# A two-block transformer on one core: the last 32 tokens of the expert layer gathered row by row, the others computed densely

## The reference, cut to what matters

```python
s1 = einsum('thd,nd->thn', q[..., :half], k1)      # 8 heads, 128 keys on each side
s2 = einsum('thd,nd->thn', q[..., half:], k2)
v1, i1 = top_k(s1, 16);  v2, i2 = top_k(s2, 16)
sc, pos = top_k(all sums v1 + v2, 16)
eidx = (i1 * 128 + i2)[pos]                        # one of 16384 experts
g = softmax(sc)
a = einsum('thkd,td->thk', expert_u[eidx], h)
out = einsum('thk,thkd->td', gelu(a) * g, expert_v[eidx])
```

## Time and profile before

| | us |
|---|---|
| device time, median of 3 runs | 1415.27 |
| lowest and highest of them | 1412.72, 1416.08 |
| device time of the profiled execution | 1414.68 |
| its span | 1412.6 |
| PE busy | 1383.5 (98%) |
| DVE busy | 1006.8 (71%) |
| ACT busy | 692.0 (49%) |
| POOL busy | 392.5 (28%) |

### The profile page before, as it was taken

One profiled execution on the slowest core, in us unless ns is written; L12 is line 12 of the kernel. 1 busy time (PEld: TensorE's weight loads), 2 busy tenths in 40 slices (PEclk: granted clock), 3 DMA queues, 4 the chain that ended last, 5 costly groups with the idle time before them and its releaser, 6 DMA issues.

```text
span 1412.6 us, 28033 instructions
## 1 busy us (share of the span) xinstructions
PE 1383.5 (98%) x11486; PEld 1357.0 (96%) x11486; DVE 1006.8 (71%) x2242; ACT 692.0 (49%) x1188; POOL 392.5 (28%) x185
## 2 busy tenths in 40 slices
PE   6999999999999999999999999999999999999998
PEld 6989899999999999999999999999999899999988
DVE  3573525859998898999966666776667954788743
ACT  5563446544454444444443333333345766656653
POOL 3744467678600000000000000000000553674332
PEclk9998999999999999999999999999999999999999
DMA  8433345555565444444455766556655534555553
GB/s 284 141 103 105 105 133 180 169 165 182 180 204 168 150 149 150 150 149 150 150 174 187 239 184 190 190 185 192 186 188 180 163 122 137 177 165 179 174 171 104
DMA packets 65095, 234.99 MB, mean 166 GB/s; under 512 B 7228, under 2 KB 7612, under 8 KB 64968
## 3 DMA queue, kind: packets, MB, share of 16 engines
q1 hardware_dynamic: 64968, 233.20, 51.8%
HBM read 232.13 MB, written 1.05 MB: 165 GB/s over the span
## 4 chain that ended last, share of the span: by engine, by line
PE 85%; DVE 9%; ACT 4%; issue 1%; DMA 0%; POOL 0%; SPq 0%; DVEq 0%; ACTq 0%
PE PS L551 84%; ACT SPL L991 2%; DVE SPL L1372 2%; DVE ub L2026 2%; DVE ub L2022 1%; DVE ub L2019 1%; PE PS L673 1%; DMA RAW<-in_dense 0%; DVE HF L1389 0%; DVE RS L1384 0%; DVE HS L1394 0%; DVE sb L1953 0%; ACT HS L1016 0%; DVE PS L1415 0%; DVE cosr L1915 0%
## 5 line engine op out<-in xcount | busy, mean ns | idle before, releaser
L991 ACT ACTIVATE SPL<-RAW 128x1024 fp32r<-128x1024 f32 x432 | 456.4, 1058 | 565.3 <-PE PS L551 561.9
L2049 POOL TENSOR_TENSOR SPL<-RAW,SPL 128x1024 fp32r<-128x1024 f32 x149 | 361.0, 2426 | 1000.8 <-ACT SPL L991 1000.7
L551 PE MATMUL PS<-HS,SPL 128*128 128x256 f32 x4656 | 572.8, 282 | 12.8 <-DVE SPL L1372 11.9
L551 PEld LDWEIGHTS PS<-HS,SPL 128*128 128x128 f32 x4656 | 554.2, 188 | 17.2 <-issue 15.7
L1372 DVE TENSOR_TENSOR SPL<-RAW,SPL 128x1024 fp32r<-128x1024 f32 x283 | 352.0, 1245 | 224.2 <-ACT SPL L991 223.1
L551 PE MATMUL PS<-asp,SPL 128*128 128x256 f32 x3072 | 358.7, 279 | 0.0
L551 PEld LDWEIGHTS PS<-asp,SPL 128*128 128x128 f32 x3072 | 358.5, 188 | 0.1
L551 PE MATMUL PS<-HXb,SPL 128*128 128x256 f32 x720 | 89.6, 285 | 1.9 <-DVE SPL L1372 1.3
L551 PEld LDWEIGHTS PS<-HXb,SPL 128*128 128x128 f32 x720 | 87.1, 189 | 3.1 <-DVE SPL L1372 2.1
L1750 DVE TENSOR_SCALAR oh<-CC,T3f 128x128 f32<-128x128 f32 x256 | 87.6, 342 | 0.0
L1749 DVE TENSOR_SCALAR oh<-CC,T3f 128x128 f32<-128x128 f32 x256 | 72.0, 281 | 0.0
(11 more groups left out here) (253 smaller groups left out, 1175.6 us busy)
## 6 DMA issues: line engine op xcount, KB each, us to landing
RAW<-in_dense SPq DMA_DIRECT2D x176, 512.0 KB, 3.6
RAW<-in_eu SPq DMA_DIRECT2D x128, 512.0 KB, 3.5
RAW<-in_ev SPq DMA_DIRECT2D x128, 512.0 KB, 4.2
bias<-in_nab SPq DMA_DIRECT2D x2, 768.0 KB, 8.3
XT<-in_xT SPq DMA_DIRECT2D x4, 256.0 KB, 5.5
out_y<-HF SPq DMA_DIRECT2D x4, 256.0 KB, 2.4
c<-in_c SPq DMA_DIRECT2D x1, 960.0 KB, 6.9
c<-in_c SPq DMA_DIRECT2D x1, 512.0 KB, 5.4
```

Source lines behind the costliest of these rows:

```text
L551: return e.matmul(out, l, r, start=start, stop=stop, skip_group_check=skip)
L991: e.activation(spl(n)[0], raw(n), ACT.Copy).then_inc(*up("act_high", ("hi", n)))
L2049: e.tensor_tensor(lo, raw(n), hi.bitcast(f32), ALU.subtract).then_inc(*up("pool_low", ("lo", n)))
```

## The change

For the expert layer the 256 tokens are divided. The first 224 (W) go the old way, with 224 columns for all U and V matmuls, 56 gate groups in place of 64 over the same 76 U steps. The last 32 (TG) are done by gathering. Transfer j, an indirect DMA on POOL's queue, brings to partition 32g + t the row of 4 KB that token t's choice 32g + j names (g from 0 to 3), so there are 32 transfers of 128 rows for u and 32 for v. DVE multiplies the u rows by the tokens' activations and sums each row (`dot`), ACT makes gelu times gate of the 128 results, and DVE adds the v rows times that onto `yrow`. At the last V step 8 small plain f32 matmuls (`fold`) add the four groups of `yrow` into the accumulators on PE. Each of the two kinds has two buffers.

The diff, cut to its core:

```diff
+TG = 32
+W = T - TG
 def low_on_dve(n):
+    if EXPERT + ROUTED + 2 <= n < EXPERT + NE:
+        return False
 def peer_steps():
-    for m in range(T // 4):
+    for m in range(W // 4):
         yield "g", m
-        while (u - ROUTED) * (T // 4) < (m + 1) * BESIDE:
+        while (u - ROUTED) * (W // 4) < (m + 1) * BESIDE:
+def gather_slots():
+    return {j * 107 // (TG - 1): j for j in range(TG)}
...
 # PE
-                        t = mm3(ps[:, 0:256], (hi[:, c, :], lo[:, c, :]), rhs_h(c), c == 0, c == 7)
+                        t = mm3(ps[:, 0:W], (hi[:, c, :], lo[:, c, :]), (HS[:, 0, c, 0:W], HS[:, 1, c, 0:W]), c == 0, c == 7)
+                    if i in (8, 9):
+                        ps = take("scr", "xrow", i - 8)
+                        for c in range(4):
+                            t = mm(ps[:, c * 128:c * 128 + 128], copies[:, 4 * (i - 8) + c, :], ident)
+                        w.wait_ge(*at("yrow", TG - 1))
+                        for c in range(8):
+                            mm(o, yrow[:, c * 128:c * 128 + 128], con("fold"), False, False, True)
...
 # ACT
+                    if i - 1 in beside:
+                        w.wait_ge(*at("dot", j))
+                        e.activation(hrow[:, j:j + 1], hrow[:, j:j + 1], ACT.Gelu)
+                        e.activation(hrow[:, j:j + 1], hrow[:, j:j + 1], ACT.Copy, scale=grow[:, j:j + 1])
+                elif what == "a":
+                    e.activation(asp[i % 4][:, 0:W], GB[:, i, :], ACT.Copy)
-                if f < 21:
-                    step()
+                step()
...
 # DVE
+                    w.wait_ge(*at("selected"))
+                    chosen()
...
+                    w.wait_ge(*at("full", "xrow", 1))
                     marks(0)
+                    if i in beside:
+                        w.wait_ge(*at("urow", j))
+                        e.scalar_tensor_tensor(u_, u_, 1.0, xrow, ALU.mult, ALU.mult, accum_out=hrow[:, j:j + 1])
+                    if i - 2 in beside:
+                        w.wait_ge(*at("vrow", j))
+                        w.wait_ge(*at("hrow", j))
+                            t = e.scalar_tensor_tensor(yrow, vrow[j % 2], hrow[:, j:j + 1], yrow, ALU.mult, ALU.add)
-                    parts(asp[i % 4][:, 0:256], asp[i % 4][:, 256:512], GB[:, i, :], ("apart", i))
+                    low_of(asp[i % 4][:, 0:W], asp[i % 4][:, 256:256 + W], GB[:, i, :], ("apart", i))
...
                 if what == "pair":
                     rstd(3)
-                    step()
-                    step()
+                    rp = bank(7)[:, 256:512]
+                    e.tensor_copy(rp, RS)
-                        e.tensor_tensor(dst, dst, RS, ALU.mult)
+                        e.tensor_tensor(dst, dst, rp, ALU.mult)
+                    step()
+                    step()
...
 # POOL
+            def gather(j):
+                if j >= 2:
+                    w.wait_ge(*at("dot", j - 2))
+                e.indirect_dma_start(urow[j % 2], None, A["er"], rows_)
+                if j >= 2:
+                    w.wait_ge(*at("yrow", j - 2))
+                e.indirect_dma_start(vrow[j % 2], None, A["ev"].rearrange("a b c -> (a b) c"), rows_)
+                if (what, i) == ("u", ROUTED + 12):
+                    gather(0)
+                if (what, i) == ("v", 0):
+                    for j in range(1, TG):
+                        gather(j)
```

More of the change, by code:

```diff
@@ L33 @@
 _at = 0
-for _n, _w in (("ident", 128), ("iota", 128), ("permd", 128), ("permr", 128)):
+for _n, _w in (("ident", 128), ("iota", 128), ("permd", 128), ("permr", 128), ("fold", TG)):
     C0[_n] = (_at, _w)
@@ L276, in build @@
         top_.take("gap0", 8)
+        ar = Arena()
+        rows1 = ar.take("rows1", 2048)
+        ar.close()
         HSt = top_.take("HS", 4096, f32r)
@@ L333, in build @@
         T3f = ex.take("T3f", 768).rearrange("p (b t) -> p b t", b=3)
+        rows = ex.take("rows", 2048)
+        xrow, yrow = rows[:, 0:1024], rows[:, 1024:2048]
+        copies = yrow.rearrange("p (c m) -> p c m", c=8)
+        urow = [ex.take("urow", 1024), rows1[:, 0:1024]]
+        vrow = [ex.take("vrow", 1024), rows1[:, 1024:2048]]
+        hrow, grow, erow = RS[:, 0:TG], RS[:, TG:2 * TG], RS[:, 2 * TG:3 * TG].bitcast(u32)
         ar = Arena()
-        GB = ar.take("GB", NE * 256).rearrange("p (i t) -> p i t", t=256)
+        GB = ar.take("GB", NE * W).rearrange("p (i t) -> p i t", t=W)
         ar.close()
         ar = Arena()
-        ar.take("first", 58 * 256)
+        ar.take("before", ROUTED * W)
         keysT = ar.take("keysT", 256).rearrange("p (a n) -> p a n", a=2)
@@ L1185, in act_program @@
                                      ACT.Copy).then_inc(*up("act_copy", ("ev", "sc", c4, a)))
+            beside = gather_slots()
             for what, i in peer_steps():
@@ L1199, in act_program @@
                         e.activation(sel[:, 2], sel[:, 2], ACT.Exp).then_inc(*up("act_exp", ("expg",)))
+                    if i == 6:
+                        w.wait_ge(*at("hn", 1, 7))
+                        e.activation(copies.rearrange("p c (g t) -> p c g t", g=GROUPS),
+                                     HF[:, :, W:T].unsqueeze(2).to_broadcast([128, 8, GROUPS, TG]),
+                                     ACT.Copy).then_inc(*up("act_copy", ("copies",)))
+                    if i in (9, 10):
+                        w.wait_ge(*at("full", "xrow", i - 9))
+                        e.activation(xrow[:, 512 * (i - 9):512 * (i - 9) + 512], psum("xrow", i - 9),
+                                     ACT.Copy).then_inc(*up("act_copy", ("ev", "xrow", i - 9)))
+                elif what == "a":
+                    w.wait_ge(*at("gated4", W // 4 - 1))
+                    w.wait_ge(*at("ev", "u", i))
+                    if i >= 4:
+                        w.wait_ge(*at("v", i - 4))
+                    e.activation(asp[i % 4][:, 0:W], GB[:, i, :], ACT.Copy).then_inc(*up("act_part", ("ahi", i)))
                 elif what == "v":
@@ L1203, in act_program @@
                     cur[0] += 1
+                    if i - 1 in beside:
+                        j = beside[i - 1]
+                        w.wait_ge(*at("dot", j))
+                        e.activation(hrow[:, j:j + 1], hrow[:, j:j + 1], ACT.Gelu).then_inc(*up("act_row", ("hgelu", j)))
+                        w.wait_ge(*at("hgelu", j))
+                        e.activation(hrow[:, j:j + 1], hrow[:, j:j + 1], ACT.Copy,
+                                     scale=grow[:, j:j + 1]).then_inc(*up("act_row", ("hrow", j)))
                     if i == NE - 8:
@@ L1752, in marks, with chosen @@
                 q.then_inc(*up("dve_mark", ("marks", m)))
+            def chosen():
+                for g in range(GROUPS):
+                    c = slice(TG * g, TG * g + TG)
+                    r = slice(TG * g, TG * g + TG)
+                    e.scalar_tensor_tensor(erow[r, 0:TG], sel[128 - TG:128, 1, 1, c], 128.0, sel[128 - TG:128, 0, 1, c],
+                                           ALU.mult, ALU.add).then_inc(*up("dve_pick", ("erow",)))
+                    e.tensor_copy(grow[r, :], sel[128 - TG:128, 2, 1, c]).then_inc(*up("dve_pick", ("grow",)))
             def gated(m):
@@ L1832, in dve_program @@
                     cur[0] += 1
+                    if i in beside:
+                        j = beside[i]
+                        w.wait_ge(*at("urow", j))
+                        w.wait_ge(*at("ev", "xrow", 1))
+                        u_ = urow[j % 2]
+                        e.scalar_tensor_tensor(u_, u_, 1.0, xrow, ALU.mult, ALU.mult,
+                                               accum_out=hrow[:, j:j + 1]).then_inc(*up("dve_row", ("dot", j)))
+                    if i - 2 in beside:
+                        j = beside[i - 2]
+                        w.wait_ge(*at("vrow", j))
+                        w.wait_ge(*at("hrow", j))
+                        if j == 0:
+                            t = e.tensor_scalar(yrow, vrow[0], hrow[:, 0:1], None, ALU.mult)
+                        else:
+                            w.wait_ge(*at("yrow", j - 1))
+                            t = e.scalar_tensor_tensor(yrow, vrow[j % 2], hrow[:, j:j + 1], yrow, ALU.mult, ALU.add)
+                        t.then_inc(*up("dve_row", ("yrow", j)))
                     if i >= NE // 2:
@@ L2156, in _constants @@
     put(c0, C0, "ident", np.eye(128))
+    put(c0, C0, "fold", p[:, None] % TG == np.arange(TG)[None, :])
     put(c0, C0, "iota", np.arange(128)[None, :])
```

44 lines of the change are left out of this document (28 added, 16 removed).

## The result

The changed kernel takes 1418.86 us (median of seven runs, 1418.64 to 1420.43), the kernel before in the same comparison 1412.91 (seven runs, 1412.14 to 1416.75). The ratio is 1.0037, with a 95% interval of 1.0025 to 1.0049. So it is slower, as forecast, and the time lies in the range, but the loss is 5.2 us by the ratio (5.9 by the medians) in place of the 11 that were forecast: about half of it. The profiled execution has a span of 1416.8 us against 1412.6.

The account below looks back on a forecast made before the run. PE, busy for 98% of the span, was taken as the bound. 1412.6 - 14.9 + 0 + 27.6 - 2.7 - 0.3 + 0 + 1.8 = 1424.1 us of span, with 2.1 outside it, gave 1426 us; range 1378 to 1455.

Parts of the forecast that it names:

- the gate phase: Beside the gates: DVE marks and POOL low parts exclude each other; 298 us, +27.6 us (+10 to +63).
- U 0 to 47: First U steps: DVE's work on the choices sets the turn, so no net gain; 0 us (-3.6 to +5).
- Rival B: Gate phase: marks and low parts don't hold each other, PE stays the bound; 1383 us, chance 0.20.
- The floor of 280.1: Gate phase minimum in us: 76 low parts of 2.40 plus 54 groups' marks of 1.81, never overlapping.
- third of the way: Gate phase: 298 us, chosen between the 280.1 us floor and 333 us if products didn't overlap low parts either.
- would cost still more: Gate phase: said of one mark getting done for each low part, as from 264.58 us; no size given.
- The pitch: V and U 124 to 127: matmuls of 224 columns start 112 ns apart, not 116.7; -14.9 us (0 to -21).
- Rivals C, D and E: Pitch stays 116.7, 1441 us, 0.12; neither lock nor pitch, 1406 us, 0.04; 224 columns like plain f32, over 1500, 0.02.
- the lower price of 106.7 ns: V and U 124 to 127: the skill's weight load sets the matmul pitch; -31.7 us in place of -14.9.
- Sine and cosine, w_down: Factor in PSUM ends PE's 2.68 us wait, -2.7 us (0 to -2.7); earlier high part in w_down, -0.3.
- Gathers: V phase: the gathers and their work on DVE, ACT and POOL cost nothing; 0 us, upper end +95.
- rival G: V phase: issuing gathers holds DVE or POOL; +58 us on the forecast, 1484 us (1448 to 1521), chance 0.10.

Follow-up runs that it names:

- e1: Changed kernel with the low parts of U 50 to 127 back on DVE; 1381.7 us, 0.9764 of the kernel before.
- e2: Changed kernel, low parts left on POOL, marks comparing with a copy of the index row in PSUM; 1382.45 us, 0.9771 of the kernel before.
- e3: Kernel before with only the low parts of U 50 to 127 moved to POOL; 1458.1 us (one run).
- the width experiment: Kernel before with matmuls in V alone at 256 down to 64 columns, another width for each 16 steps; 1438.3 us.
- e8: Kernel of e1 with block 2's two low parts ahead of sine and cosine again, factor still from PSUM; 1378.44 us, 0.9744 of the kernel before.
- e10: Kernel before with only sine and cosine taking their factor from PSUM, behind the two low parts; 1410.63 us, ratio 0.9969.
- e4: Changed kernel without the gathers and the work on their rows; 1419.7 us (one run), V 345.00 us.
- e9: Kernel of e8 with the CAST for the high part of asp in V back on DVE; 1378.8 us (one run).

## Why the prediction was wrong in size

The change in the span was forecast as +11.5 us and is +4.2. Three terms failed: the size of the gate phase (6.3 us too high), U 0 to 47 taken as nothing (3.3 too high) and the gain at sine and cosine (3.3 too low). The time lies in the range, but that range was 77 us wide.

**The gate phase: right in its mechanism, too high by 6.3 us.** Forecast +27.6 (298 us), measured +21.3 (290.3). e1, e2 and e3 show the lock from three sides: take away POOL's part, take away DVE's SBUF operand, or put POOL's part into the kernel before. Rival B is refuted by all three.

The step that failed is the list of what stands one behind another, in the floor and in the ceiling. The floor of 280.1 added all marks to all low parts, but a held mark gets done inside the hold: 75 marks must come off it, 17 us. And it counted nothing for the products into GB, on the ground that they run beside POOL. They can, but they stand in one queue behind a held mark, and mostly run once it is over. By the counts of the trace, 76 low parts of 2.40 are 182.4 us and 357 marks outside at 0.226 are 80.7, which leaves 27.2 of the 290.3 us. The trace gives the time outside POOL's low parts directly, 105.6 us: marks take 74.3 of it, products 22.7 (another 14.4 us of products run beside a low part), the ends of held marks 6.8, and all else under 2. The two errors partly cancelled and left the floor 10.2 us too low. Then the "third of the way" to a ceiling in which all eight marks and all products lie outside the low parts added 18 and brought 298, 7.7 us too many (of which 1.3 are offset, since the phase before took 269.1 and not 270.4). That the miss is not larger is in part luck.

In e3 the same count is 182.4 + 421 x 0.226 = 277.5, and 35.6 us of the 313.1 are left; its products, larger with 256 tokens, take 34.0 us outside the low parts, and scaling by the ratio of the floors missed that. One sign in the prediction was read the wrong way round: that one mark gets done for each low part "would cost still more". It is what happened (75 marks, 76 low parts), and it saves time against the floor's way of counting, since that mark needs none of its own. The ceiling's own sum gives 334 us, not 333, which changes nothing.

**The pitch: right.** 112 assumed, 111.7 measured, by the changed kernel's V (-13.5 us with `fold`, where -14.9 x 128/132 + 1.8 = -12.6 was forecast: 5.0 ns saved by each of 3072 matmuls, not 4.7) and by the width experiment. Rivals C, D and E are out, and so is the lower price of 106.7 ns. The Trainium skill, "TensorE: Matmul & The Clock Gate", section "Back-to-back issue gap", leaves the spacing to both instructions of a pair, and its section "LDWEIGHTS (loading the stationary operand)" makes 106.7 ns of a load of 128 columns (an estimate, 128/1.2). The width experiment never goes below 111.7.

**U 0 to 47: forecast 0, measured -3.3 us.** The step that failed was "DVE's work on the choices sets the turn". The choices were done at 430.2 us in place of 433.9, PE's turn came 4.1 us sooner, and of this only the 0.8 us were given back that PE waits for the first marks. Before, DVE waited 1.9 us in this phase for ACT's high parts; with the faster PE they come sooner, and the changed trace has none of these waits. Where the rest of the 3.7 us comes from no run was made to show. `chosen` takes the 1.3 us that were forecast, but behind the turn.

**Sine and cosine, w_down: forecast -3.0, measured +0.3.** The prediction named it in its range, "the moved low part could be late instead", and took the better end. The mechanism that took the gain is the one on which its largest term rests: an instruction with two SBUF inputs beside POOL's low part is held. It was applied to sine and cosine and not to the low part that came behind them. At that place the wait of 2.68 us became one of 1.72, a low-clock stretch of 13 matmuls behind it cost 1.2 us, and the 160 weight loads there take 0.5 us more than before. e8 and e10 show that the 2.7 us were there to be had with the order as before. The earlier high part in w_down wasn't tried alone; the 0.36 us for which the weight loads waited there are gone from the changed kernel's trace, and so is a low-clock stretch of 10 matmuls that the kernel before has there. One loss stood in no sum and stays open: between the two places every kernel with the change loses 0.9 us (193.2 in place of 192.3), and not by a wait but load by load. A stretch of 164 weight loads on `mixT` has a mean distance of 122.3 ns in place of 119.1, and in w_down it is 118.7 in place of 116.7, for the same matmuls of 256 columns; in e10, whose only edit is on DVE, it is 117.8. No run shows why.

**Gathers: 0, right** (e4, e9); rival G falls. The Trainium skill, "SBUF — State Buffer", warns in its section "SBUF: two separate sides" of descriptors that can't be written while DVE runs a two-port instruction. In e9 a CAST from SBUF to SBUF stands in each V step, and neither V (345.01 us) nor POOL's time for a transfer (1.1 us) differs from e8's, so this case does not show the effect; only 12 transfers were issued beside such an instruction, and longer casts were not tried.

In the sum of the span: -6.3 from the gates, -3.3 from U 0 to 47, +3.3 from the tail and about -1 from V and the steps around it make the 7.3 us between 1424.1 and 1416.8.

**Low-clock stretches.** In these traces a stretch at the low clock in w_down (10 to 27 matmuls) or behind the wait in block 2 (11 to 15) is there in some executions and not in others, at 0.1 us a matmul. The seven times of the changed kernel lie at 1418.6 to 1418.9 and at 1420.1 to 1420.4; a stretch of 15 matmuls is just the 1.5 us between. That it is this in each of them is inferred, since only one has a trace.

## What to carry to other kernels

Before moving work from DVE to POOL, look at what stays on DVE. In these traces a tensor_scalar or a cast from SBUF to SBUF, and a two-input instruction with both inputs in SBUF, waits until the POOL instruction that it meets has ended, so some 90 us of low parts taken off DVE left it busier than before. Give such an instruction an operand in PSUM, or leave the work where it is; and when an instruction is moved in time, ask of the moved one, too, whether it now starts inside a POOL instruction. As long as DVE has slack, holds cost almost nothing, and then each of them counts (7 us for half of them, 37 for all), so a part of a move can look harmless.
